# Weights stored in the order of their transfers: a decoder trunk with 352 MB of expert weights on one core

## The reference, cut to what matters

```python
D_MODEL, SEQ, D_FF, N_EXPERTS, TOP_K, D_FF_EXPERT = 1024, 256, 2816, 8, 2, 3584

def swiglu(h, w1, w3, w2):
    return (jax.nn.silu(h @ w1) * (h @ w3)) @ w2

def moe_swiglu(h, router, w1, w3, w2):
    logits = (h @ router).astype(F32)
    top_v, top_i = lax.top_k(logits, TOP_K)
    gates = jax.nn.softmax(top_v, axis=-1)
    dense_gate = jnp.sum(jax.nn.one_hot(top_i, N_EXPERTS, dtype=F32) * gates[..., None], axis=-2)
    y = jnp.zeros(h.shape, F32)
    for e in range(N_EXPERTS):
        y = y + swiglu(h, w1[e], w3[e], w2[e]).astype(F32) * dense_gate[..., e:e + 1]
    return y.astype(h.dtype)
```

## Time and profile before

| | us |
|---|---|
| median of 3 runs | 1428.12 |
| lowest and highest | 1422.86, 1428.26 |
| the profiled execution, its own time | 1424.22 |
| its span on the page | 1422.4 |
| TensorE busy | 1343.2 (94%) |
| DMA queue of SP: share of the 16 engines' span | 77.7% |
| mean rate over the span | 305 GB/s |

### The profile page before, as it was taken

One profiled execution on the slowest core, in us unless ns is written; L12 is line 12 of the kernel. 1 busy time (PEld: TensorE's weight loads), 2 busy tenths in 40 slices (PEclk: granted clock), 3 DMA queues, 4 the chain that ended last, 5 costly groups with the idle time before them and its releaser, 6 DMA issues.

```text
span 1422.4 us, 16931 instructions
## 1 busy us (share of the span) xinstructions
PE 1343.2 (94%) x6926; PEld 851.2 (60%) x6926; DVE 483.3 (34%) x816; ACT 395.6 (28%) x623; POOL 79.7 (6%) x68
## 2 busy tenths in 40 slices
PE   7999999999999999999999999989889889889887
PEld 5777888888878687445888535344344344334343
DVE  1618277777634635303988100100100100100002
ACT  3244254444423414113777111111011011011012
POOL 0262000000005400000000000000000000000000
PEclk9999999999999999999999999999999999999998
DMA  9530723652372128699999999999999999999996
GB/s 321 206 118 32 264 89 136 220 178 90 130 274 98 60 81 348 273 417 406 415 417 392 352 417 410 412 419 409 412 419 408 412 418 410 412 417 410 412 417 259
DMA packets 120490, 433.54 MB, mean 305 GB/s; under 512 B 5726, under 2 KB 30452, under 8 KB 113268
## 3 DMA queue, kind: packets, MB, share of 16 engines
q1 hardware_dynamic: 120244, 432.25, 77.7%
q0 software_dynamic: 192, 0.53, 0.1%
HBM read 431.71 MB, written 1.05 MB: 304 GB/s over the span
## 4 chain that ended last, share of the span: by engine, by line
PE 64%; SPq 19%; DMA 11%; DVE 4%; issue 1%; ACT 1%; DVEq 0%; ACTq 0%
SPq L539 19%; PE bank L2048 15%; DMA ring<-in_moe_w 10%; PE bank L2127 8%; PE bank L1566 7%; PE bank L1953 5%; PE bank L1571 5%; PE bank L1589 4%; PE bank L2062 3%; PE bank L1957 3%; PE bank L1552 1%; PE bank L1843 1%; PE bank L1844 1%; PE bank L1850 1%; PE bank L1538 1%
## 5 line engine op out<-in xcount | busy, mean ns | idle before, releaser
L2048 PE MATMUL bank<-ring,xs 128*64 128x512 f32 x1568 | 350.7, 596 | 34.8 <-DMA ring<-in_moe_w 34.8
L2048 PEld LDWEIGHTS bank<-ring,xs 128*64 128x64 f32 x1568 | 108.3, 137 | 253.8 <-issue 199.6
L2048 PE MATMUL bank<-ring,s_act 128*64 128x512 f32 x784 | 178.0, 597 | 20.1 <-DMA ring<-in_moe_w 20.1
L1448 DVE TENSOR_TENSOR s_act<-wsT,bank 128x256 f32<-128x256 f32 x49 | 20.6, 421 | 511.0 <-ACT wsT L866 511.0
L2048 PEld LDWEIGHTS bank<-ring,s_act 128*64 128x64 f32 x784 | 56.7, 137 | 124.7 <-issue 122.7
L1953 PE MATMUL bank<-x_both,wf_hi 128*128 128x512 f32 x336 | 118.8, 395 | 0.0
L866 ACT ACTIVATE wsT<-bank 128x256 f32<-128x256 f32 x49 | 18.8, 383 | 343.5 <-PE bank L2062 343.5
L1566 PE MATMUL bank<-xnT,ring 128*128 128x256 f32 (+2 forms) x448 | 102.6, 388 | 0.6 <-ACT bias L710 0.6
L1481 DVE TENSOR_TENSOR ring_lo<-ring,w_hi 128x2048 fp32r<-128x2048 f32 (+1 forms) x44 | 95.6, 2192 | 18.0 <-ACT w_hi L933 17.8
L796 ACT ACTIVATE wf_hi<-ring 128x1024 fp32r<-128x1024 f32 x66 | 69.8, 1060 | 98.6 <-PE bank L1953 67.5
L1957 PE MATMUL bank<-x_both,wf_lo 128*128 128x256 f32 x336 | 94.1, 280 | 0.0
(11 more groups left out here) (359 smaller groups left out, 1610.5 us busy)
## 6 DMA issues: line engine op xcount, KB each, us to landing
ring<-in_moe_w SPq DMA_DIRECT2D x168, 2048.0 KB, 23.2
ring<-in_ffn_w SPq DMA_DIRECT2D x18, 1536.0 KB, 6.7
ring<-in_w_in SPq DMA_DIRECT2D x6, 2048.0 KB, 15.3
ring<-in_w_out SPq DMA_DIRECT2D x8, 1024.0 KB, 4.9
ring<-in_ffn_w SPq DMA_DIRECT2D x3, 2048.0 KB, 7.8
ring<-in_w_in SPq DMA_DIRECT2D x4, 1024.0 KB, 15.7
ring<-in_xa_wkv SPq DMA_DIRECT2D x2, 2048.0 KB, 15.1
ring<-in_w_in SPq DMA_DIRECT2D x2, 1184.0 KB, 6.7
```

Source lines behind the costliest of these rows:

```text
L2048: i = mm(dst[SMALL * side:SMALL * side + SMALL, :], rows, ring[:, s, at:at + FC], start=opens, stop=closes)
```

## The change

The host now lays the weights out anew. `pack_experts` makes one array `experts[8][21][128][4096]`: for each expert and each unit, what each partition is to hold, as 4096 consecutive floats. `pack_weights` does the same in one flat array `packed` for the units of both layers and of the SwiGLU; the table `PACKED` has the place of each. The two loaders on SP then move, for each unit, one run per partition. Which weights lie where in a slot, the ring, its waits, the order of the transfers and their number are as before, and no instruction of TensorE, VectorE, ScalarE or GpSimd is touched.

```diff
+def rows_on_partitions(block):
+
+    rows, cols = block.shape
+    return np.ascontiguousarray(block.reshape(rows // P, P, cols).swapaxes(0, 1)).reshape(-1)
...
+def pack_experts(inputs):
+
+    out = np.empty((N_EXP, len(JOB_UNITS), P, 4096), np.float32)
+    for e in range(N_EXP):
+        for u, (w, d, part) in enumerate(JOB_UNITS):
+            if w == 2:
+                r0 = CHUNK0[d] + FC * part
+                out[e, u] = inputs["moe_w2"][0, e, r0:r0 + FC, :].reshape(P, 4096)
+            else:
+                width = CHUNKS[d] * FC
+                rows = 4096 // width * P
+                block = inputs[f"moe_w{w}"][0, e, rows * part:rows * part + rows, CHUNK0[d]:CHUNK0[d] + width]
+                out[e, u] = rows_on_partitions(block).reshape(P, 4096)
+    return out
...
+                def packed(name, *at):
+
+                    lo, hi = PACKED[name, *at]
+                    return A["packed"][lo:hi].rearrange("(p n) -> p n", p=P)
+
...
                 for s, (lo, hi) in enumerate(IN_UNITS):
-                    unit(0, s, ring[:, s, 0:KT * (hi - lo)].rearrange("p (k c) -> p k c", k=KT),
-                         A["w_in"][lay, :, lo:hi].rearrange("e (k p) c -> p (e k) c", p=P))
+                    unit(0, s, ring[:, s, 0:KT * (hi - lo)], packed("in_units", layer, s))
...
-                unit(1, U_WKV, v3(ring[:, U_WKV, :], 0, 4096, KT),
-                     A["xa_wkv"][lay].rearrange("e (k p) c -> p (e k) c", p=P))
...
+                unit(1, U_WKV, ring[:, U_WKV, :], packed("wkv", layer))
...
+                    for u in range(3 * len(FFN_TILES)):
+                        unit(2 + u // RING, slot_of(u), ring[:, slot_of(u), 0:FFN_TILES[u // 3] * D], packed("ffn", u))
...
-                    width = CHUNKS[d] * FC
-                    if w == 2:
-                        r0 = CHUNK0[d] + FC * part
-                        dst, src = v3(slot, 0, 4096, 4), A["moe_w2"][0, ex, r0:r0 + FC, :]
-                    else:
-                        rows = 4096 // width * P
-                        dst = v3(slot, 0, 4096, 4096 // width)
-                        src = A[f"moe_w{w}"][0, ex, rows * part:rows * part + rows, CHUNK0[d]:CHUNK0[d] + width]
-                    rows_by = "e (p k) c -> p (e k) c" if w == 2 else "e (k p) c -> p (e k) c"
-                    sp.dma_start(dst, src.rearrange(rows_by, p=P)).then_inc(arrived[slot_of(u)], 16)
+                    sp.dma_start(slot, A["experts"][ex, u].rearrange("e p n -> p (e n)")).then_inc(arrived[slot_of(u)], 16)
```

More of the change, by code:

```diff
@@ L68, with packed_blocks, pack_weights @@
 FFN_WHERE = [(c, k, n) for c, n in enumerate(FFN_TILES) for k in range(n)]
+def packed_blocks():
+    for layer in range(DEPTH):
+        for s, (lo, hi) in enumerate(IN_UNITS):
+            yield ("in_units", layer, s), "w_in", layer, (0, D), (lo, hi)
+        yield ("wkv", layer), "xa_wkv", layer, (0, D), (0, 2 * GW)
+        for i, m in enumerate(WOUT_ORDER):
+            yield ("wout", layer, i), "w_out", layer, (256 * m, 256 * m + 256), (0, D)
+        yield ("wq", layer), "xa_wq", layer, (0, D), (0, GW)
+        yield ("wo", layer), "xa_wo", layer, (0, GW), (0, D)
+    for c, n in enumerate(FFN_TILES):
+        f0 = P * sum(FFN_TILES[:c])
+        for w, name in enumerate(("ffn_w1", "ffn_w3")):
+            yield ("ffn", 3 * c + w), name, 0, (0, D), (f0, f0 + n * P)
+        yield ("ffn", 3 * c + 2), "ffn_w2", 0, (f0, f0 + n * P), (0, D)
+def rows_on_partitions(block):
+    rows, cols = block.shape
+    return np.ascontiguousarray(block.reshape(rows // P, P, cols).swapaxes(0, 1)).reshape(-1)
+def pack_weights(inputs):
+    return np.concatenate([rows_on_partitions(inputs[name][index, r0:r1, c0:c1])
+                           for _, name, index, (r0, r1), (c0, c1) in packed_blocks()])
+def pack_experts(inputs):
[11 more added lines that the diff above has]
+    return out
 def slot_of(u):
@@ L136 @@
 WOUT_ORDER = (1, 0, 3, 2)
+PACKED, _at = {}, 0
+for _key, _, _, (_r0, _r1), (_c0, _c1) in packed_blocks():
+    PACKED[_key] = (_at, _at + (_r1 - _r0) * (_c1 - _c0))
+    _at = PACKED[_key][1]
 R_MIX, R_XA, R_MEM, R_FFN, R_BA, R_PB, R_PS, R_SB, N_ROWS = 0, 8, 16, 24, 32, 33, 35, 37, 41
@@ L501, in _ @@
                               .then_inc(S["loaded_mem"], 16)
-                unit(1, U_WKV, v3(ring[:, U_WKV, :], 0, 4096, KT),
-                     A["xa_wkv"][lay].rearrange("e (k p) c -> p (e k) c", p=P))
[L504 to L510, removed]
-                if layer < 1:
[L512 to L521, removed]
+                unit(1, U_WKV, ring[:, U_WKV, :], packed("wkv", layer))
+                for i in range(4):
+                    unit(1, U_WOUT + i, ring[:, U_WOUT + i, 0:2048], packed("wout", layer, i))
+                unit(1, U_WQ, ring[:, U_WQ, 0:2048], packed("wq", layer))
+                unit(1, U_WO, ring[:, U_WO, 0:2048], packed("wo", layer))
+                if layer < 1:
+                    for u in range(3 * len(FFN_TILES)):
+                        unit(2 + u // RING, slot_of(u), ring[:, slot_of(u), 0:FFN_TILES[u // 3] * D], packed("ffn", u))
             def job_loads(j, e):
@@ L2175, in _ @@
             combine(n_jobs)
-INPUTS = ("x", "mem", "rel_bias", "final_norm", "norm_mix", "w_in", "gla_wa2", "gla_ba", "gla_norm", "pool_w", "pool_b",
-          "pool_scale", "sgu_ln_g", "sgu_ln_b", "sgu_w", "sgu_b", "w_out", "norm_xa", "norm_mem", "xa_wq", "xa_wkv",
-          "xa_wo", "norm_ffn", "ffn_w1", "ffn_w3", "ffn_w2", "router", "moe_w1", "moe_w3", "moe_w2")
+INPUTS = ("x", "mem", "rel_bias", "final_norm", "norm_mix", "gla_wa2", "gla_ba", "gla_norm", "pool_w", "pool_b",
+          "pool_scale", "sgu_ln_g", "sgu_ln_b", "sgu_w", "sgu_b", "norm_xa", "norm_mem", "norm_ffn", "router")
 def kernel(**inputs):
@@ L2190 @@
     arrays = {name: _np.ascontiguousarray(inputs[name]) for name in INPUTS}
+    arrays["packed"], arrays["experts"] = pack_weights(inputs), pack_experts(inputs)
     for name, value in zip(("consts", "glam", "onehot", "flip"), shape_constants()):
```

## The result

| | before | changed |
|---|---|---|
| median, us | 1425.49 (4 runs, 1422.84 to 1428.26) | 1404.00 (4 runs, 1402.67 to 1404.45) |
| the profiled execution, its own time | 1424.22 | 1404.45 |
| its span | 1422.4 | 1402.6 |

The ratio is 0.9847, with a 95% interval of 0.9821 to 0.9874: faster by 1.5%. Between the two profiled executions lie 19.8 us, in their own times and in their spans.

What follows compares the result with a forecast made beforehand. The prediction held that expert loads set the last five jobs' pace, 106.55 us where TensorE needs 92.5. Gains of 18.2 + 1.5 = 19.8 us gave 1404.4 from the profiled 1424.2, 1406.1 from the mean; forecast 1406, range 1400 to 1413.

Steps and rivals of the forecast that it cites:

- Where loads count: After the start, TensorE waits for loads only at the experts' matmuls: 46 times, 54.9 us; none in layers or dense SwiGLU.
- the restart: Expert loads, held up by the full job's slots, resume full rate at about 802 us; this point was to stay.
- The price of a unit by its form: Expert unit: 4.90 us in 16 KB runs, 5.12 in 4 KB, 5.41 in 2 KB; 9 ns a run.
- rival 2: Half the gain: a longer stretch of such expert units settles at 5.0 us each; 1416 or 1418 us; chance 5%.
- How many units: 118 expert units count after 802 us: five whole jobs and the last 13 units of the third; gain 19.8 us.
- The sum of 19.8 us: Gain in the late expert jobs: 18.2 us from five jobs plus 1.5 from the third; ends 17.5 and 20.9.
- TensorE next: In late jobs TensorE, 92.5 us a job, gains 10.4 on loads and waits again from about 960 us; nothing lost.
- Layers, SP, the tail, the instruction queue at 0: Layers' units, SP's issuing, the tail after 1392.03 us and delayed instruction fetches each change nothing; 2 us kept for fetches.
- The rule against the rows: For DMA packets, the skill's 3.5 ns overhead gives about 8 us gain; the trace's 9 ns a run was used instead.
- Rivals 1 and 3: Expert loads: 1, engines' ceiling, 4.83 us a unit, 1398 us, 4%; 3, transfers split in 4 KB pieces, 1424 to 1428, 4%.
- The number given: Whole kernel: 1406 us predicted, from 1404.4 by the profiled execution and 1406.1 by the mean of four known times.
- Rival 4, memory conflicts: Expert loads: aligned 16 KB pattern conflicts in memory, slowing units to 5.41 us; 1463 us; chance 3%.

Runs made afterwards that it cites:

- e2_layers_only: The changed kernel with the experts' loads turned back, so only the layers' and dense SwiGLU's units are packed; 1424.56 us, ratio 1.0001 to the kernel before.
- e1_experts_only: The kernel before with only the experts' loads replaced by packed ones; 1404.09 us, ratio 0.9844 to the kernel before.
- e9_full_third: The changed kernel with one small job put before the full job, which becomes third instead of second; 1398.23 us, ratio 0.9803 to the kernel before.
- e8_pitch_20k: The changed kernel with 4 KB of padding after each partition's 16 KB, so partitions read 20 KB apart; 1403.40 us, ratio 0.9852 to the kernel before.
- e3_runs_4k: The changed kernel with 256 B of padding after each 4 KB, so all expert units have 4 KB runs; 1430.78 us, ratio 1.0036 to the kernel before.
- e5_runs_2k: The changed kernel with 256 B of padding after each 2 KB, so all expert units have 2 KB runs; 1475.17 us, ratio 1.0347 to the kernel before.
- e6_runs_8k: The changed kernel with 256 B of padding after each 8 KB, so all expert units have 8 KB runs; 1413.79 us, ratio 0.9916 to the kernel before.

## Why the prediction was right

Point by point, by its own steps.

- *Where loads count.* Waits for loads only in the experts, from the restart on: `e2_layers_only` (1.0001) and `e1_experts_only` (0.9844) show both halves of it.
- *The price of a unit by its form.* 4.90 us was read from the `w2` units; all 21 units now take 4.894. Fours in a row were enough to know what 118 in a row do, so rival 2 falls. The 9 ns a run, which had been fitted to three lengths, held for a fourth.
- *How many units.* 118, and a restart that stays: the third job started 0.43 us later. (The count stopped at 1404 us, while the loads ran on at 414 GB/s to about 1406.6; with that it is 119, as in the expectations, and 0.2 us more.) The sum of 19.8 us was the difference of the profiled executions to the tenth, 1404.4 against 1404.45. So exact a hit is luck: a job became 3.77 us shorter and not 3.65, 0.6 us more over five jobs, and the later third job and a tail that was 0.2 us longer took it back. The pace alone had left 17.5 to 20.9.
- *TensorE next.* 92.5 us a job against 102.8: it stayed second. Its waits fell to 36.1 us, with 35 forecast. The first of them was placed at about 960 us. It is seen at 941:

```profile
941.29 3.65 PE L2082 MATMUL bank<-ring,xs 128*64 128x512 f32 x16 [0.99 <-DMA ring<-in_experts]
```

  The step that failed is the even rate by which TensorE was to catch up, 10.4 us a job. Within a job it is uneven: in the middle a unit takes TensorE 3.4 us and it gains 1.5 on each load; at the end, with turns and gathers between, it loses. It touches the loads first in the middle of a job. This changed no sum here, but it is half of what made the estimate for `e9_full_third` wrong; the other half is the splitting.
- *Layers, SP, the tail, the instruction queue at 0.* All held. If 16 KB packets delayed instructions, `e2_layers_only` should be slower than before, for its layers have such packets beside them; and the third job, whose weights now come in such packets alone, still took TensorE 92.5 us. The waits for the instruction queue were not looked at one by one.
- *The rule against the rows.* The Trainium skill (DMA: Bandwidth & Descriptors, Why small descriptors are slow) allowed a gain of 8 us as an estimate, by the fixed overhead per packet alone; the rows' 9 ns a run gave 19.8, and this was measured. The same section has a second cost that the prediction left out, 32 bytes of descriptor for each operation. At the trace's 428 / 16 = 26.8 GB/s an engine that would be 1.2 ns more, as an estimate, and 4.7 ns in all are still half of what the runs show.
- *Rivals 1 and 3.* The rate ends at 428 GB/s, and 4.83 us a unit would be 434. Of the 37,418 packets 27,830 are of 8 KB and more, so the transfers are not split in 4 KB pieces.
- *The number given.* 1406 was 2.0 above the measured median. The 1.6 us that I added for the difference between the profiled execution and the other runs were not needed: the first runs of the kernel before had been high. Its 14 runs beside `e1_experts_only` have a median of 1424.65, close to its profiled 1424.22. The changed kernel's four runs lie within 1.8 us, and its median is 0.45 under its profiled execution.
- *Rival 4, memory conflicts.* 428 GB/s over 570 us refutes it, and `e8_pitch_20k` shows that a distance of 16 KB or of 20 KB between partitions makes no difference.

## What to carry to other kernels

Where the DMA engines are what ends last, look for the transfer of the longest runs in the trace: in this kernel its pace was what the others could have, once the data lay in the order of the transfers. Count only the bytes after the last point at which the queue ran dry for another reason, and nothing for loads that nobody waits for. For buffers, compare lateness at its worst within a stage, not the mean pace of the stage, and ask what has to be done between a landing and its first use.

## What the runs showed of the hardware beside that

**SP's long issues were no cause.** In the kernel before, the chain gave SP's issuing 19% of the span, and one issue took up to 15.6 us. With 4 KB runs everywhere (`e3_runs_4k`) the issues look so (minimum, median and maximum in ns), and the chain gives SP 34%:

```profile
L575 SPq DMA_DIRECT2D ring<-in_experts x168: 539/4707/5901, 524.4 to 1390.0; - x168
```

In the changed kernel they look so, and the chain gives SP 0%:

```profile
L573 SPq DMA_DIRECT2D ring<-in_experts x168: 327/333/609, 524.9 to 1356.3; - x168
```

In both the queue never runs dry in the late jobs (a share of 1.03 and 1.01), and both lie on the same line of 9 ns a run. A reader of the chain alone would have laid a fifth of the kernel on SP. With short runs SP waits inside the issue when the queue is full. In `e3_runs_4k` the first three issues into the empty queue take about 0.6 us each and the fourth 4.7; in `e5_runs_2k`, with 2 KB runs, the five from 579.8 to 597.8 us take 0.54 us each, while the rate is already 387 GB/s. And with 8 KB runs (`e6_runs_8k`), which lie on the same line, the median issue is 0.54 us and the chain gives SP 0%. So the 9 ns are not SP's. What the queue is full of (its number of runs, say) was not tested.

**What lies between runs of one kernel.** The profile of `e1_experts_only` has a span of 1405.2 us, 2.6 more than the changed kernel. Its later pace is the same (428 GB/s). Most of the difference is there at 60 us, where the same step of TensorE's program stands 2.2 us later (61.72 against 59.55), and it stays: the third job starts at 797.20 against 794.93. Two stretches of ten microseconds, first of the changed kernel, then of this one:

```profile
26.00:36.00 10.00, 10.00 (x66) 7.32 (x64) 0.90 (x4) 5.15 (x13) 0.77 (x1) 0.83 0.99 416
36.00:46.00 10.00, 8.49 (x56) 7.71 (x55) 6.39 (x16) 3.43 (x9) 2.08 (x3) 1.00 0.99 422
```
```profile
26.00:36.00 10.00, 10.00 (x47) 7.04 (x45) 0.39 (x2) 3.83 (x10) 0.77 (x1) 0.70 1.08 377
36.00:46.00 10.00, 8.49 (x65) 7.33 (x65) 4.84 (x14) 4.75 (x12) 2.08 (x3) 0.96 1.07 375
```

Up to 30 us the granted clock is 1.00 in both, with TensorE busy from about 11 us on. Then it falls to the lower of its two levels (1.2 and 2.4 GHz; windows of 1 us read 0.50) and comes back. A mean of 0.83 over 10 us is 3.4 us at half the clock; 0.70 and then 0.96 are 6.8 us. As an estimate, 3.4 us more at half the clock cost 1.7 us. The kernel before has 0.83 there at 376 GB/s, so it is not the faster layers' loads that spare the changed kernel. The rest is in the first 32 matmuls on the tokens (L1586), which took 5.51 us in the changed kernel and 6.66 here, at a granted clock of 1.00 in both; why is open. They began 0.5 us earlier here.

The record of all runs points the same way. Of the 14 runs of the kernel before beside `e1_experts_only`, the two with a mean granted clock of 0.996 took 1422.8 and 1423.0 us, the three with 0.995 1423.7 to 1424.2, the two with 0.992 1427.4 and 1427.7, and of the seven with 0.993 six took 1424.2 to 1425.2, one 1427.9. The four runs of `e8_pitch_20k` do the same: three at 0.996 within 0.6 us, and one at 0.992 with 1408.12. So the clock goes along with the spread of a kernel's runs; no run set it, so this is read and not tested. Between kernels, differences of a microsecond or two mean little unless the clocks are alike.
